# Sliding attention units in a two-block kernel: the parts of one unit lie more steps apart

## The reference

```
q, k, v = _split_cols(h @ w_in, ODD_SIZES)          # 16 query heads, 4 key/value heads, 64 wide
q = _rms_norm(q.reshape(b, s, C_HEADS, HEAD_DIM), qn_c)
k = _rms_norm(k.reshape(b, s, C_KV_HEADS, HEAD_DIM), kn_c)
...
logits = jnp.einsum('bnqhgd,bnkhd->bnhgqk', qb, kk) * HEAD_DIM ** -0.5   # 128 queries, 256 keys
logits = logits - sl[None, None, :, :, None, None] * dist
logits = jnp.where(valid[None, :, None, None], logits, -jnp.inf)
p = jax.nn.softmax(jnp.concatenate([logits, sink], axis=-1), axis=-1)[..., :-1]
out = jnp.einsum('bnhgqk,bnkhd->bnqhgd', p, vv)
```

## Time and profile before

| | |
|---|---|
| median of 3 runs | 3396.25 us (3395.53 to 3400.5) |
| the profiled execution | 3395.65 us |
| its span in the trace | 3393.9 us |
| PE busy, share of the span | 2895.9 us, 85% |
| DVE | 1336.2 us, 39% |
| ACT | 983.6 us, 29% |
| POOL | 1267.9 us, 37% |
| DMA | mean 78 GB/s |
| chain that ended last | PE 72%, DVE 20%, issue 3%, ACT 2%, POOL 2% |

### The profile page before, as it was taken

One profiled execution on the slowest core, in us unless ns is written; L12 is line 12 of the kernel. 1 busy time (PEld: TensorE's weight loads), 2 busy tenths in 40 slices (PEclk: granted clock), 3 DMA queues, 4 the chain that ended last, 5 costly groups with the idle time before them and its releaser, 6 DMA issues.

```text
span 3393.9 us, 33284 instructions
## 1 busy us (share of the span) xinstructions
PE 2895.9 (85%) x12679; PEld 2312.3 (68%) x12679; DVE 1336.2 (39%) x1816; ACT 983.6 (29%) x1532; POOL 1267.9 (37%) x574
## 2 busy tenths in 40 slices
PE   4766569899999778999989976599999977799998
PEld 3645347688787556887878974477887754478876
DVE  6559863232203763222025225503221199532211
ACT  2112232233323453332223322223332211333321
POOL 1211659234443102444423445333444333134442
PEclk7777665899999998999989987799999988899999
DMA  7421223223323101223222210022332211023321
GB/s 218 152 84 62 72 90 112 70 79 99 96 83 82 38 26 50 80 93 96 90 64 87 88 63 1 0 75 75 99 99 84 78 62 37 25 75 99 95 82 59
DMA packets 271419, 264.47 MB, mean 78 GB/s; under 512 B 20844, under 2 KB 270285, under 8 KB 271309
## 3 DMA queue, kind: packets, MB, share of 16 engines
q1 hardware_dynamic: 271309, 262.96, 24.7%
HBM read 260.85 MB, written 2.10 MB: 77 GB/s over the span
## 4 chain that ended last, share of the span: by engine, by line
PE 72%; DVE 20%; issue 3%; ACT 2%; POOL 2%; SPq 0%; DMA 0%; DVEq 0%; POOLq 0%; ACTq 0%
PE bank L1008 18%; PE bank L1009 18%; PE bank L1010 18%; DVE v_cm L1924 5%; DVE ada_acc L2097 2%; PE bank L1060 2%; PE bank L1047 1%; PE bank L1049 1%; PE bank L1048 1%; PE bank L1083 1%; PE bank L1032 1%; PE bank L1326 1%; PE bank L1033 1%; DVE root L2030 1%; PE bank L1034 1%
## 5 line engine op out<-in xcount | busy, mean ns | idle before, releaser
L698 POOL TENSOR_TENSOR w_lo<-w_raw,w_hi 128x1024 fp32r<-128x1024 f32 (+1 forms) x408 | 968.0, 2385 | 1873.3 <-ACT w_hi L1532 1311.2
L1008 PE MATMUL bank<-h_hi,w_hi 128*128 128x512 f32 x1888 | 752.0, 398 | 91.9 <-DVE u_pad L1931 30.3
L1009 PE MATMUL bank<-h_lo,w_hi 128*128 128x512 f32 x1888 | 745.1, 395 | 0.0
L1010 PE MATMUL bank<-h_hi,w_lo 128*128 128x512 f32 x1888 | 744.2, 394 | 0.0
L1008 PEld LDWEIGHTS bank<-h_hi,w_hi 128*128 128x128 f32 x1888 | 361.0, 191 | 176.3 <-issue 69.3
L1532 ACT ACTIVATE w_hi<-w_raw 128x1024 fp32r<-128x1024 f32 (+1 forms) x232 | 232.4, 1013 | 646.8 <-PE bank L1010 624.0
L1009 PEld LDWEIGHTS bank<-h_lo,w_hi 128*128 128x128 f32 x1888 | 361.3, 191 | 76.1 <-issue 1.7
L1010 PEld LDWEIGHTS bank<-h_hi,w_lo 128*128 128x128 f32 x1888 | 360.8, 191 | 76.6
L2124 DVE TENSOR_TENSOR tmp<-sq,bank 128x512 f32<-128x512 f32 x88 | 60.6, 689 | 699.8 <-PE bank L1010 699.8
L1008 PE MATMUL bank<-a_hi,w_hi 128*128 128x512 f32 x704 | 282.6, 401 | 21.6 <-DVE a_lo L2128 21.6
L1009 PE MATMUL bank<-a_lo,w_hi 128*128 128x512 f32 x704 | 276.8, 393 | 0.0
(11 more groups left out here) (307 smaller groups left out, 3954.1 us busy)
## 6 DMA issues: line engine op xcount, KB each, us to landing
ada_w<-in_ada_w_dram SPq DMA_DIRECT2D x48, 512.0 KB, 6.4
w_raw<-in_ffn_gate_dram SPq DMA_DIRECT2D x22, 1024.0 KB, 5.3
w_raw<-in_ffn_up_dram SPq DMA_DIRECT2D x22, 1024.0 KB, 5.3
w_raw<-in_ffn_w_gate_dram SPq DMA_DIRECT2D x22, 1024.0 KB, 5.3
w_raw<-in_ffn_w_up_dram SPq DMA_DIRECT2D x22, 1024.0 KB, 5.3
w_raw<-in_ssm_w_in_dram SPq DMA_DIRECT2D x20, 1024.0 KB, 5.2
w_raw<-in_ada_w_dram SPq DMA_DIRECT2D x16, 1024.0 KB, 5.1
w_raw<-in_ffn_down_dram SPq DMA_DIRECT2D x16, 1024.0 KB, 5.2
```

Source lines behind the costliest of these rows:

```text
L698: pool.tensor_tensor(w_lo[parity][:, 0:nk, half], w_raw[parity][:, 0:nk, half], w_hi[parity][:, 0:nk, half].bitcast(F32), ALU.subtract).th ...
L1008: pe.matmul(dst[m][:], hi, src_hi(k0 + k), start=first and k == 0, stop=False)
L1009: pe.matmul(dst[m][:], hi, src_lo(k0 + k), start=False, stop=False)
L1010: ins = pe.matmul(dst[m][:], lo, src_hi(k0 + k), start=False, stop=last and k == nk - 1)
```

## The change

The distances become: scores 0, turn 2, tile_back 7, weigh 4 on TensorE; round_y 8, copy 2, exponential 0 on ScalarE; low_y 8, scale_y 5, least_of 0 on VectorE. In each step TensorE puts one query part between scores and turn, and the second (where there is one) between tile_back and weigh. o_pt and o_ytok have three buffers instead of two. The loops have two more steps.

```
--- before.py
+++ after.py
@@ -233,8 +233,8 @@
         oy_lo = in_big("oy_lo", [P, 8, S], 36, F32R)
         o_neg = [in_big(f"o_neg{j}", [P, S], 52 + 2 * j) for j in range(3)]
         o_prob = [in_big(f"o_prob{j}", [P, S], 58 + 2 * j) for j in range(4)]
-        o_pt = [in_big(f"o_pt{j}", [P, S], 66 + 2 * j) for j in range(2)]
-        o_ytok = [in_big(f"o_ytok{j}", [P, P], 70 + 0.5 * j) for j in range(2)]
+        o_pt = [in_big(f"o_pt{j}", [P, S], 66 + 2 * j) for j in range(3)]
+        o_ytok = [in_big(f"o_ytok{j}", [P, P], 72 + 0.5 * j) for j in range(3)]
 
         a_hi = in_big("a_hi", [P, FC, S], 0, F32R)
         a_lo = in_big("a_lo", [P, FC, S], FC * S * 4 / KB, F32R)
@@ -908,7 +908,7 @@
                 for t_ in range(2):
                     for q in range(nb):
                         at = P * (nb * t_ + q)
-                        ins = pe.matmul(bank[b][:, HD * t_:HD * t_ + HD], o_pt[u % 2][:, at:at + P],
+                        ins = pe.matmul(bank[b][:, HD * t_:HD * t_ + HD], o_pt[u % 3][:, at:at + P],
                                         cv[:, i + 1 - nb + q, HD * (hp // 2):HD * (hp // 2) + HD],
                                         start=q == 0, stop=q == nb - 1)
                 ins.then_inc(o_weighed, 1)
@@ -919,7 +919,7 @@
                     take(7, o_ylow, U)
                 else:
                     pe.wait_ge(o_ylow, u)
-                pe.transpose(bank[7][:, 0:P], o_ytok[u % 2][:], ident[:]).then_inc(o_back, 1)
+                pe.transpose(bank[7][:, 0:P], o_ytok[u % 3][:], ident[:]).then_inc(o_back, 1)
 
             slot_cm(n0, n0 % 2, lambda k: h_hi[:, k, :], lambda k: h_lo[:, k, :],
                     [take(O_BANK[j], o_normed, j + 1) for j in range(2)], before=h_chunk(2))
@@ -936,17 +936,20 @@
             sums(4)
             half_cm(n0 + 4, 0, take(O_BANK[6], o_normed, 7))
             sums(5)
-            for s in range(U + 5):
+            for s in range(U + 7):
+                fill = list(range(o_upto(s), o_upto(s + 1)))
                 if s < U:
                     scores(s)
+                for f in fill[:1]:
+                    query_part(f)
                 if 2 <= s < U + 2:
                     turn(s - 2)
-                if 3 <= s < U + 3:
-                    weigh(s - 3)
-                if s >= 5:
-                    tile_back(s - 5)
-                for f in range(o_upto(s), o_upto(s + 1)):
+                if s >= 7:
+                    tile_back(s - 7)
+                for f in fill[1:]:
                     query_part(f)
+                if 4 <= s < U + 4:
+                    weigh(s - 4)
                 if s == 0:
                     sums(6)
                 for j in o_ends(s - 1):
@@ -1458,9 +1461,9 @@
             def copy_turned(u):
                 hp, i, w = o_tile(u)
                 act.wait_ge(o_turned, u + 1)
-                if u >= 2:
-                    act.wait_ge(o_weighed, u - 1)
-                act.activation(o_pt[u % 2][:, 0:2 * w], bank[5][:, 0:2 * w], ACT.Copy).then_inc(o_ptcopied, 1)
+                if u >= 3:
+                    act.wait_ge(o_weighed, u - 2)
+                act.activation(o_pt[u % 3][:, 0:2 * w], bank[5][:, 0:2 * w], ACT.Copy).then_inc(o_ptcopied, 1)
 
             def round_y(u):
                 hp, i, w = o_tile(u)
@@ -1486,11 +1489,11 @@
             root_of(4)
             square(6)
             root_of(5)
-            for s in range(U + 6):
+            for s in range(U + 8):
+                if s >= 8:
+                    round_y(s - 8)
                 if 2 <= s < U + 2:
                     copy_turned(s - 2)
-                if s >= 6:
-                    round_y(s - 6)
                 if s < U:
                     prob_exp(s)
                 if s == 0:
@@ -1988,9 +1991,9 @@
                 link(dve.tensor_tensor(tt, tt, sink_exp[:, e:e + 2], ALU.add))
                 link(dve.reciprocal(pinv[:, e:e + 2], tt))
                 dve.wait_ge(o_weighed, u + 1)
-                if u >= 2:
-                    dve.wait_ge(o_back, u - 1)
-                dve.tensor_tensor(o_ytok[u % 2][:].rearrange("p (h e) -> p h e", e=HD),
+                if u >= 3:
+                    dve.wait_ge(o_back, u - 2)
+                dve.tensor_tensor(o_ytok[u % 3][:].rearrange("p (h e) -> p h e", e=HD),
                                   bank[6][:, 0:P].rearrange("p (h e) -> p h e", e=HD),
                                   pinv[:, e:e + 2].unsqueeze(2).to_broadcast([P, 2, HD]), ALU.mult).then_inc(o_yscaled, 1)
 
@@ -2002,13 +2005,13 @@
 
             for j in range(6):
                 normed(j)
-            for s in range(U + 6):
-                if 4 <= s < U + 4:
-                    scale_y(s - 4)
+            for s in range(U + 8):
+                if s >= 8:
+                    low_y(s - 8)
+                if 5 <= s < U + 5:
+                    scale_y(s - 5)
                 if s < U:
                     least_of(s)
-                if s >= 6:
-                    low_y(s - 6)
                 if s == 1:
                     normed(6)
                 for j in o_ends(s - 2):
```

## The result

| | before | after |
|---|---|---|
| median, 20 runs each | 3397.93 us | 3403.42 us |
| profiled span | 3393.9 us | 3400.5 us |
| mean granted clock, whole span | 0.887 | 0.882 |

The ratio is 1.0016, 95% interval 1.0009 to 1.0023: 5.5 us slower (3.1 to 7.8). The forecast was +1.7 us.

What follows compares the result with a forecast made beforehand. Bound before: a TensorE-VectorE loop in the second layer's sliding attention; after: VectorE and ScalarE taking turns. Terms 2.3 - 3.3 - 0.3 + 3 = +1.7 us on the median 3396.25 gave 3398.0 us, range 3387 to 3408.

Steps and rivals of the forecast that it cites:

- part 1: TensorE in the attention stage: leaves the loop, its work of about 3.5 us a step becoming a floor, not the bound.
- part 2: VectorE and ScalarE: low part waits for rounding issued behind the exponentials, so they take turns, 3.88 us a plain turn.
- part 3: ScalarE's projection work comes onto the path: square and rounding add 1.44 us, root with table load 1.97, giving 5.85.
- part 4: GpSimd's weight rounding holds VectorE's sum L1988 behind each square, adding 1.87 us; that turn takes 7.2.
- The clock term: Whole stage: TensorE idling in long turns and running at the lower clock, +3 us, ends 0 and +12.
- class sum: Units 8 to 31: 23 turns summed by kind (squares, roots, inversions, plain), less one-block units, 118.7 us.
- rival A: Slower: plain turns behind squares, roots and inversions run at TensorE's lower clock, about 7 us each, +11; 3406 us, chance 0.20.
- its own sign: Test for rival A: granted clock of 1160 to 1280 us falls under about 0.85.
- The drain: From the last minimum to the last low part, 11.3 us before: -0.3, ends -2 and +2.
- unit 0 to 8: Start of the stage, before low parts are due: -2.2 and -1.1, together -3.3 us.
- the loop: Units 8 to 31: 118.7 us against 116.4 before, +2.3, with the clock's +3 put separately on the stage.
- Rival C: Much faster: coupling of rounding and exponentials doesn't bind, steps run at 3.5 us, 22 us go; 3376 us, chance 0.05.

Runs made afterwards that it cites:

- experiment 1: Changed kernel, ScalarE issuing the high part of unit s-7 ahead of the exponentials of unit s; 3371.43 us, 0.9927 of the kernel before.
- experiment 5: Kernel before, with only ScalarE's high part moved behind the exponentials; 3443.02 us, 1.0142 of the kernel before.
- experiment 2: Changed kernel, the two-column sum in scale_y made two instructions with a scalar operand; 3398.83 us, 1.0008 of the kernel before.
- experiment 4: Changed kernel, TensorE repeating the scores product three or four more times for some of units 10 to 22; 3399.72 us, 1.0009 of the kernel before.
- Experiment 8: Changed kernel, one step less of distance (weigh 3, scale 4, tile back 6, high and low part 7); 3399.48 us, 1.0009 of the kernel before.
- experiment 6: Changed kernel, all query parts put back at the end of a TensorE step, behind the weighing; 3413.90 us, 1.0053 of the kernel before.
- the fastest kernel here: experiment 1 with TensorE repeating the scores product three more times for units 12, 17, 22 and 26; 3365.84 us, 0.9911 of the kernel before.

## Why the prediction was right, and where its sizes were off

- That TensorE leaves the loop (part 1) was right: VectorE's wait for scores is 3.2 us of 35.7. That TensorE's own wait for the low part would mostly vanish was not: 22.8 us of 30.2 are left, but TensorE now has that time in hand.
- That VectorE and ScalarE take turns because the high part is issued behind the exponentials (part 2) was right in mechanism and size, 3.87 for 3.88. Experiments 1 and 5 show the cause from both sides: put ahead, 32 us come off changed by the medians (30 by the ratios); put behind in the kernel before, 47 us are added.
- The price of squares and roots on the path (part 3) was right: 7.2 and 5.9 us.
- The meeting with GpSimd (part 4) was right: 2.05 us measured for 0.15 + 1.87, and it goes when a scalar operand stands in place of the second tensor (experiment 2). By the rule of the Trainium skill (SBUF — State Buffer, "Who interferes with whom") a VectorE instruction with two SBUF inputs had to be hit under a GpSimd instruction that reads SBUF. The trace agrees, four times in four.
- The clock term was +3 for the whole stage. From unit 8 to 31 the measured time exceeds the class sum by 123.0 - 118.7 = 4.3 us, and experiment 4 gave back 4.9, of which 3.6 lie behind its repeats: inside the term's ends of 0 and 12. The mechanism of rival A was there, and its own sign too: the granted clock fell to 0.83, under its 0.85. What it had wrong was the price of 11 us: the slow plain turns took 4.0 to 5.3 us and not 7. An argument for that, which no run tests, is that ScalarE has some time in hand: it sat idle 2.04 us ahead of the exponentials of unit 31.
- The drain was mis-sized. I took -0.3 and it came +3.0. I held that three buffers let the turned tiles run ahead. But bank 6 is single: weighings and scalings stay a chain, 2.4 us a unit at the lower level and 1.6 at the high one (experiment 1), and a greater distance leaves one unit more in it. Experiment 8 gives 1.6 us of the 3.0 to that distance. For the rest there are two candidates, the lower clock and the first low part, which comes 1.3 us later by the same turn-taking as in part 2; no run takes them apart.
- What I didn't see is experiment 6: the new place of the parts was priced at nothing, and it saves 10 us of the changed kernel, mostly by letting the sums and so the root start early. The comparison with before held all the same, since the turns were worked out for the order as it stands.
- In sum the stage came 4.0 us over its forecast of +1.7: unit 0 to 8 0.6 us lower, the loop 1.3 higher and the drain 3.3 higher, so the drain is most of what the number missed. The measured 3403.42 us lies just above the 3403.0 beyond which I had put 0.22; against 3397.93 of the kernel before it is 5.5 us, within the 6.8 that I took as no change.
- Rival C (steps of 3.5 us, 3376) named the kernel of experiment 1, not this one: what stood in its way was the order of two calls on ScalarE.

## What to carry to other kernels

Making the distances between the parts of a unit larger took TensorE out of the loop here and still gained nothing, because on ScalarE one producer was left directly in front of its consumer. Write down for each wait what stands ahead of the producer in its own queue, here the exponentials of the unit just finished. Where an engine must wait once in each step, put its independent work inside that wait: that alone gave 15 of the 30 us of the fastest kernel here. A stage with a single bank between two engines pays its chain for each unit that is still to drain, here 1.6 us for one step of distance.

## What the runs showed of the hardware

A VectorE instruction of two elements a partition took 2.05 us instead of 0.15 under a GpSimd instruction that reads SBUF, and with a scalar operand in place of the second tensor 0.23 us, in the middle of the same GpSimd instruction. Repeated products that nobody needs, placed in TensorE's waits, raised the granted clock of a stretch of 122 us from 0.83 to 0.95, and the turns behind them were 3.6 us shorter in all; placed on the path once, they cost 3.9 us in a single turn. The same drain of dependent small instructions took 9.6 us at a granted clock of 0.86 and 11.3 at 0.63, and that of experiment 1 10.3 us at 0.87 and 12.3 at 0.65.
